# Two column groups in an output projection, staging rows on whole lines, and an expert stage's begin and end rearranged

## What is computed

```python
def _gated_head_norm(o, gate, w):
    of = o.astype(f32)
    y = of * lax.rsqrt(jnp.mean(of * of, axis=-1, keepdims=True) + EPS)
    return y * w.astype(f32) * jax.nn.silu(gate.astype(f32))
...
    o = _gated_head_norm(o, og.reshape(b_, L, H_A, DV_A), gnorm_w)
    return o.reshape(b_, L, DVT_A).astype(h.dtype) @ w_out, S_f, S_b
```

```python
        u = jnp.take(u_tab, idx, axis=0)
        act = jax.nn.gelu(jnp.einsum('td,ted->te', hc, u), approximate=False)
        coef = gates.astype(hc.dtype) * act
        vv = jnp.take(v_tab, idx, axis=0)
        return jnp.einsum('te,ted->td', coef, vv)
```

## Time and profile before

| | us |
|---|---|
| median of 3 runs (4644.31 to 4648.92) | 4647.11 |
| profiled execution | 4647.06 |
| its span | 4645.2 |
| span: mix_out layer 0, layer 1 | 730.6 to 855.3, 2914.3 to 3030.9 |
| span: experts layer 0, layer 1 | 1230.5 to 2452.7, 3406.6 to 4627.1 |
| PE busy | 4146.5 (89%) |
| DVE busy | 3803.5 (82%) |
| POOL, ACT busy | 1991.1 (43%), 1642.9 (35%) |

### The profile page before, as it was taken

The page is one execution under the profiler, slowest core; times in us unless marked ns, Lnnn a source line. Parts: engine busy times, 40 slices in busy tenths (PEclk is TensorE's granted clock), DMA queues, the critical chain, the costliest instruction groups (busy, mean ns, idle before and its releaser), DMA issues. The chain is left out here.

```text
span 4645.2 us, 72467 instructions
## 1 busy us (share of the span) xinstructions
PE 4146.5 (89%) x24511; PEld 3755.6 (81%) x24511; DVE 3803.5 (82%) x6733; ACT 1642.9 (35%) x2307; POOL 1991.1 (43%) x1435
## 2 busy tenths in 40 slices
PE   7799986877799999999996888786889999999997
PEld 3599986875699999999986778785779999999996
DVE  7688884599788888999996876378978888899997
ACT  7545442213233333333334432221323333333333
POOL 3234331215454545566544221220744545565663
PEclk9899998888899999999997988897999999999998
DMA  9411112214999999999972110220699999999995
GB/s 368 146 46 55 54 33 74 60 31 91 270 366 360 364 360 358 366 362 362 363 281 81 38 40 20 82 66 16 148 316 363 362 362 363 356 365 363 361 361 207
DMA packets 616027, 1049.49 MB, mean 226 GB/s; under 512 B 229699, under 2 KB 388870, under 8 KB 615430
## 3 DMA queue, kind: packets, MB, share of 16 engines
q1 hardware_dynamic: 467814, 508.86, 32.4%
q0 software_dynamic: 147456, 536.94, 31.1%
q10 hardware_dynamic: 672, 2.62, 0.2%
HBM read 982.75 MB, written 65.54 MB: 226 GB/s over the span
## 5 line engine op out<-in xcount | busy, mean ns | idle before, releaser
L1920 POOL DMA_INDIRECT rows_ex<-in_peer_v,ctx_index x512 | 707.6, 1382 | 475.5 <-DVE row_acc_ex L1999 359.9
L1920 POOL DMA_INDIRECT rows_ex<-in_peer_u,ctx_index x512 | 588.0, 1148 | 645.4 <-DVE dots_ex L2002 501.7
L2088 PE MATMUL pu_ex<-h_hi,uT_hi_ex 128*128 128x384 f32 x2048 | 715.6, 349 | 1.9 <-ACT coef_ex L1944 1.0
L1999 DVE SCALAR_TENSOR_TENSOR row_acc_ex<-rows_ex,factor_ex,row_acc_ex 128x1024 f32<-128x1024 f32 x512 | 657.6, 1284 | 52.8 <-issue 11.1
L2088 PE MATMUL pu_ex<-h_hi,uT_lo_ex 128*128 128x384 f32 x2048 | 692.6, 338 | 0.0
L2088 PE MATMUL pu_ex<-h_lo,uT_hi_ex 128*128 128x384 f32 x2048 | 692.5, 338 | 0.0
L2096 PE MATMUL py_ex<-v_hi_ex,c_hi_ex 128*128 128x512 f32 x1536 | 622.4, 405 | 0.0
L2002 DVE CUSTOM_DVE_ANT_0 rows_ex<-rows_ex,h_row_ex 128x1024 f32<-128x1024 f32 x512 | 604.3, 1217 | 0.0
L2096 PE MATMUL py_ex<-v_lo_ex,c_hi_ex 128*128 128x512 f32 x1536 | 601.0, 391 | 0.0
L2096 PE MATMUL py_ex<-v_hi_ex,c_lo_ex 128*128 128x512 f32 x1536 | 600.6, 391 | 0.0
L1933 ACT ACTIVATE uT_hi_ex<-pT_ex 128x512 fp32r<-128x512 f32 x512 | 304.1, 594 | 575.1 <-PE pT_ex L2081 473.0
(11 more groups left out here) (418 smaller groups left out, 8599.6 us busy)
## 6 DMA issues: line engine op xcount, KB each, us to landing
u_raw_ex<-in_peer_u SPq DMA_DIRECT2D x256, 512.0 KB
v_raw_ex<-in_peer_v SPq DMA_DIRECT2D x256, 512.0 KB
ada<-in_ada_w SPq DMA_DIRECT2D x24, 2048.0 KB, 10.0
gates<-stage_ro SPq DMA_DIRECT2D x12, 4096.0 KB, 23.3
g_raw_ex<-gates SPq DMA_DIRECT2D x256, 192.0 KB
w_raw_hgrn<-in_hgrn_w_in SPq DMA_DIRECT2D x40, 512.0 KB
w_raw_re<-in_peer_w_q SPq DMA_DIRECT2D x32, 512.0 KB, 3.7
w_raw_gla<-in_gla_w_in SPq DMA_DIRECT2D x25, 512.0 KB
```

What stands on the lines that cost most here:

```text
L1920: pool.indirect_dma_start(out=rows[m % RING][:, :], out_offset=None, in_=a["peer_u" if m < TG * NC else "peer_v"].rearrange("l n d -> (l n ...
L1999: nc.vector.scalar_tensor_tensor(row_acc[g][:, :], rows[j][:, :], factor[:, j:j + 1], row_acc[g][:, :], ALU.mult, ALU.add).then_inc(row_fr ...
L2088: last_ = nc.tensor.matmul(pu[:, 0:TD], w[:, k, :], x[:, k, 0:TD], start=(k == 0 and w is uT_hi[b] and x is h_hi), stop=(k == DC - 1 and w ...
```

## The change

`mix_out` takes two columns along in its loop over k instead of three. All squares and all sigmoids have buffers of their own, so the squares wait for nothing; the sums of squares, their inverses and roots are made in two groups of half the heads; there are two spread buffers, spread g + 2 standing behind head g's products. The gate's product with x and the norm weight (`gated`) is taken before the spread one, up to three chunks ahead. ACT issues all sigmoids ahead of the first root; SP loads gates 0 and 1 ahead of the weights. In `route` the `stage` buffers are allocated first. `experts` lets PE add the two parts of `h_row` by products with a rounded identity (`ident_r`, made in setup), ACT copies them, and PE's wait for that stands after the first turns. At its end the copies are shared 3 to 3 between ACT and DVE and PE starts after three of them, the turned rows have four buffers, and POOL's adds have no drain between them.

```diff
...
@@ -109,7 +109,7 @@
...
-            ("scale_w", [P, DC, 2], F32), ("lb", [P, 16], F32), ("oml", [P, 16], F32),
+            ("scale_w", [P, DC, 2], F32), ("ident_r", [P, P], F32R), ("lb", [P, 16], F32), ("oml", [P, 16], F32),
...
@@ -251,6 +251,8 @@
...
+            act.wait_ge(iot, 1)
+            act.activation(c["ident_r"][:, :], c["ident"][:, :], ACT.Copy)
...
@@ -1169,34 +1171,37 @@
...
-    AHEAD = 3
+    AHEAD = 2
+    GROUP = H // 2
...
-        sg = [sb(f"sg{i}", [P, T]) for i in range(2)]
-        sq = [sb(f"sq{i}", [P, T]) for i in range(2)]
+        sg = sb("sg", [P, DC, T])
+        sq = sb("sq", [P, DC, T])
...
-        spread_s = ps("spread_s", [P, 4, P])
-        spread_c = ps("spread_c", [P, P])
+        spread_s = [ps(f"spread_s{i}", [P, 4, P]) for i in range(2)]
+        spread_c = [ps(f"spread_c{i}", [P, P]) for i in range(2)]
...
-        rows = pp[0][0][:, 0:H * NT]
+
+        rows = [pp[j][0][:, 0:GROUP * NT] for j in range(2)]
+        inv = [c["inv"][:, j * GROUP * NT:(j + 1) * GROUP * NT] for j in range(2)]
 
         @block.sync
...
@@ -1208,10 +1213,9 @@
...
             gates(0)
+            gates(1)
             weights(0)
             weights(1)
-            gates(1)
-            weights(2)
             gates(2)
...
@@ -1228,14 +1232,11 @@
...
-            def gate(k):
+            for k in range(DC):
                 pool.wait_ge(sig_done, k + 1)
-                pool.tensor_tensor(og[:, k, :], og[:, k, :], sg[k % 2][:, :], ALU.mult).then_inc(gate_done, 1)
-
-            for k in range(DC):
-                gate(k)
-                if k < AHEAD:
-                    low(k)
+                pool.tensor_tensor(og[:, k, :], og[:, k, :], sg[:, k, :], ALU.mult).then_inc(gate_done, 1)
+                if k in (1, 2):
+                    low(k - 1)
...
@@ -1247,33 +1248,28 @@
...
-            def sigmoid(k):
+            for k in range(0, DC, 2):
+                act.activation(sq[:, k, :], oT[:, k, :], ACT.Square).then_inc(sq_act, 1)
+            for k in range(DC):
                 if k % 2 == 0:
                     act.wait_ge(og_in[k // 2], 16)
-                if k >= 2:
-                    act.wait_ge(gate_done, k - 1)
-                act.activation(sg[k % 2][:, :], og[:, k, :], ACT.Sigmoid).then_inc(sig_done, 1)
-
-            for k in range(0, DC, 2):
-                if k >= 2:
-                    act.wait_ge(summed, k - 1)
-                act.activation(sq[0][:, :], oT[:, k, :], ACT.Square).then_inc(sq_act, 1)
-            act.wait_ge(inverted, 1)
-            act.activation(inv, inv, ACT.Sqrt).then_inc(rooted, 1)
-            sigmoid(0)
-            high(0)
-            high(1)
-            sigmoid(1)
-            high(2)
-            for k in range(DC):
-                if k + 2 < DC:
-                    sigmoid(k + 2)
+                if k == 4:
+                    high(0)
+                    high(1)
+                act.activation(sg[:, k, :], og[:, k, :], ACT.Sigmoid).then_inc(sig_done, 1)
+            for j in range(2):
+                act.wait_ge(inverted, j + 1)
+                act.activation(inv[j], inv[j], ACT.Sqrt).then_inc(rooted, 1)
+                if j == 0:
+                    act.wait_ge(y_done, 1)
+                    act.activation(h_hi[:, 0, :], y[0][:, :], ACT.Copy).then_inc(hi_done, 1)
+            for k in range(1, DC):
...
@@ -1283,22 +1279,22 @@
...
         def _(pe):
-            for g in range(H):
+            def sums(g):
                 for k in range(g * NV, (g + 1) * NV):
                     pe.wait_ge((sq_act, sq_dve)[k % 2], k // 2 + 1)
                 for t in range(NT):
+                    col = g % GROUP * NT + t
                     for k in range(g * NV, (g + 1) * NV):
-                        last = nc.tensor.matmul(rows[:, g * NT + t:g * NT + t + 1], sq[k % 2][:, t * P:(t + 1) * P],
+                        last = nc.tensor.matmul(rows[g // GROUP][:, col:col + 1], sq[:, k, t * P:(t + 1) * P],
                                                 c["ones_d"][:, 0:1], start=(k % NV == 0), stop=(k % NV == NV - 1))
-                last.then_inc(summed, NV)
-            pe.wait_ge(rooted, 1)
+                last.then_inc(summed, 1)
...
             def spread(g):
-                if g:
-                    pe.wait_ge(spread_read, g)
+                pe.wait_ge(rooted, g // GROUP + 1)
                 for t in range(NT):
-                    dst = spread_s[:, t, :] if t < NT - 1 else spread_c[:, :]
-                    last = nc.tensor.matmul(dst, inv[:, g * NT + t:g * NT + t + 1].to_broadcast([P, P]),
+                    dst = spread_s[g % 2][:, t, :] if t < NT - 1 else spread_c[g % 2][:, :]
+                    col = g % GROUP * NT + t
+                    last = nc.tensor.matmul(dst, inv[g // GROUP][:, col:col + 1].to_broadcast([P, P]),
...
@@ -1310,18 +1306,24 @@
...
+            for g in range(GROUP):
+                sums(g)
             spread(0)
+            spread(1)
+            for g in range(GROUP, H):
+                sums(g)
             for k in range(DC):
-                if k % NV == NV - 1 and k // NV + 1 < H:
-                    spread(k // NV + 1)
-                if k == 0:
-                    pe.wait_ge(w_lo_done, AHEAD)
                 pe.wait_ge(lo_done, k + 1)
                 for j in range(AHEAD):
+                    if k == 0:
+                        pe.wait_ge(rooted, j + 1)
+                        pe.wait_ge(w_lo_done, j + 1)
                     for i, cols in halves():
                         last = terms(j, k, i, cols)
                         if k == DC - 1:
                             last.then_inc(proj, 1)
+                if k % NV == NV - 1 and k // NV + 2 < H:
+                    spread(k // NV + 2)
...
@@ -1332,45 +1334,55 @@
...
-            for k in range(1, DC, 2):
-                if k >= 2:
-                    dve.wait_ge(summed, k - 1)
-                nc.vector.tensor_mul(sq[1][:, :], oT[:, k, :], oT[:, k, :]).then_inc(sq_dve, 1)
-            dve.wait_ge(summed, DC)
-            nc.vector.tensor_scalar(inv, rows, float(D / mx.dv), EPS, ALU.mult, ALU.add)
-            dve.drain()
-            nc.vector.reciprocal(inv, inv)
-            dve.drain().then_inc(inverted, 1)
+            def gated(k):
+                dve.wait_ge(gate_done, k + 1)
+                nc.vector.scalar_tensor_tensor(oT[:, k, :], oT[:, k, :], c["vec"][:, gw + k % NV:gw + k % NV + 1],
+                                               og[:, k, :], ALU.mult, ALU.mult)
+
+            def inverse(j):
+                dve.wait_ge(summed, (j + 1) * GROUP)
+                nc.vector.tensor_scalar(inv[j], rows[j], float(D / mx.dv), EPS, ALU.mult, ALU.add)
+                dve.drain()
+                nc.vector.reciprocal(inv[j], inv[j])
+                dve.drain().then_inc(inverted, 1)
 
             def normal(k):
                 g = k // NV
                 dve.wait_ge(spread_done, g + 1)
-                by = (spread_s[:, :, :].rearrange("p t n -> p (t n)"), spread_c[:, :])
+                by = (spread_s[g % 2][:, :, :].rearrange("p t n -> p (t n)"), spread_c[g % 2][:, :])
                 for v, cols in parts():
-                    last = nc.vector.scalar_tensor_tensor(y[k % 3][:, cols], oT[:, k, cols],
-                                                          c["vec"][:, gw + k % NV:gw + k % NV + 1], by[v],
-                                                          ALU.mult, ALU.mult)
-                if k % NV == NV - 1:
-                    last.then_inc(spread_read, 1)
+                    last = nc.vector.tensor_tensor(y[k % 3][:, cols], oT[:, k, cols], by[v], ALU.mult)
+                last.then_inc(y_done, 1)
...
+            for k in range(1, DC, 2):
+                nc.vector.tensor_mul(sq[:, k, :], oT[:, k, :], oT[:, k, :]).then_inc(sq_dve, 1)
+            dve.wait_ge(sq_act, DC // 2)
+            dve.wait_ge(sq_dve, DC // 2)
+            gated(0)
+            gated(1)
+            inverse(0)
+            gated(2)
+            dve.drain()
             for k in range(DC):
                 normal(k)
-                dve.wait_ge(gate_done, k + 1)
-                dve.drain()
-                nc.vector.tensor_mul(y[k % 3][:, :], y[k % 3][:, :], og[:, k, :]).then_inc(y_done, 1)
+                if k == 0:
+                    inverse(1)
+                if k + 3 < DC:
+                    gated(k + 3)
                 if k >= 1:
                     low(k - 1)
+                dve.drain()
             low(DC - 1)
             dve.wait_ge(x_in, 16)
...
@@ -1577,6 +1589,7 @@
...
+        stage = [sb(f"stage{i}", [P, KEYS, STORE]) for i in range(2)]
...
@@ -1596,7 +1609,6 @@
...
-        stage = [sb(f"stage{i}", [P, KEYS, STORE]) for i in range(2)]
...
@@ -1875,14 +1887,19 @@
...
+        def turned_rows(k):
+
+
+            return (pu, pT[:, 0, :]) if k % 4 == 0 else (py[2 * (k % 4) - 2], py[2 * (k % 4) - 1])
...
@@ -1923,8 +1940,9 @@
...
                 pool.wait_ge(squared, k + 1)
```

(50 more changed lines are left out.)

19 lines of the change are left out of this document (9 added, 10 removed).

## The result

| | before | changed |
|---|---|---|
| median, us | 4647.7 | 4603.8 |
| lowest to highest | 4644.3 to 4648.9 | 4598.9 to 4607.1 |
| span of the profiled execution | 4645.2 | 4596.8 |

What follows compares the result with a forecast made beforehand. The experts' loop keeps the tensor engine busy 200 of 200 us beside a DMA share of 0.97 and stays; only stage ends move. 22 + 0.5 + 11.3 + 2.8 + 3.5 = 40.1 off 4647.11 gives 4607, own range 4601 to 4614.

Steps and rivals of the forecast that it cites:

- Route: Route's stores: aligned 256 B rows land sooner, ACT stops waiting; 11.1 and 10.6 us, sum 22, between 0 and 23.
- what ends last: Route's end, layer 0: last store lands at 1217.8, DVE's second look-up ends at 1218.2, then 1.2 for the barrier.
- The lower bound: Route's packet price: 13.6 ns for an aligned 256 B, from the projection's 512 B weight rows at 27.1 ns.
- Projection, layer 0: Output projection, layer 0: later first product, shorter turns, six columns instead of five; gain 0.5 us, between -2 and 2.5.
- Projection, layer 1: Output projection, layer 1: gates near 2926, root 2929, turns at DVE's 2.7; gain 11.3 us, between 8 and 12.
- same chain of DVE: Projection, layer 1: DVE's work between the forty sums (to 2943) and the first product, put at 2948.9.
- Rival D: Projection's loop over k: clock does not rise, turns 7.8 and 3.2, total 4635; chance 0.06.
- Experts' begin: Experts' start: 32 accumulating products at 0.217 replace DVE's adds; 1.4 us a layer, sum 2.8, between 0 and 8.
- Experts' end: Experts' end: two ACT copies instead of four, POOL's adds without drains; sum 3.5 us, up to 18.
- the drain that moves: Experts' end: the 7.3 us is paid by POOL's first drain behind the gathers, now the block's own; 1.8 gained; forecast's chance 0.46.
- the one that vanishes: Experts' end, rival A: the first drain's 7.3 us belongs to its place and goes; 14.5 more, 4592; chance 0.26.
- Rival C: Experts' loop becomes bound by DMA at a lower rate, slower than before; 4703 at 7% lower; chance 0.03.

Runs made afterwards that it cites:

- 19.2 alone: Kernel before with one edit, route's stage buffers allocated first: 4629.4 us, ratio 0.9953.
- its second: The changed kernel itself, unaltered, timed and traced once more: 4598.4 us, ratio 0.9896.
- the edit alone: Kernel before with only the output projection's (`mix_out`) edits: 4632.9 us, ratio 0.9964; looked at again, 4631.4, ratio 0.9957.
- the two kernels with `low` first: Changed kernel with DVE's low(k - 1) ahead of gated(k + 3): 4596.4 us; the same plus early drain on POOL and early first root: 4570.7.
- the experiment: Changed kernel with one more POOL drain right behind its last gather: 4590.3 us, ratio 0.9874.
- the three offset kernels: Kernel before with route's stage first but its rows 64, 128 or 224 B past a multiple of 256: 4649.1, 4648.1 and 4648.6 us.

## Why the prediction was right, point by point

The forecast 4607 stood 3 us above 4603.8, and the mechanisms of route and of the drain held. That it came so close is in part luck. Between the traces the projection gained 22.4 against 11.8 forecast, the experts 2.6 against 6.3, route 21.3 against 22, all else 2.1 against nothing: 48.4 against 40.1, of which the medians keep 43.9.

- **Route**, forecast 22, measured 21.3 in the traces, 19.2 alone. Price of a packet 13.6 forecast, 14.1 measured; store 15.4 to its landing forecast, 15.9 measured; what ends last was the pair forecast. The lower bound was taken from 512 B rows, which turned out the right neighbour.
- **Projection, layer 0**, forecast 0.5 (-2 to 2.5). Against the one trace before it gained 5.5 in the changed kernel's first trace, 2.2 in its second, -1.8 with the edit alone; against traces that entered the stage alike 5.5, 0.8 and -0.3. Two of these three lie within the bounds, and the first trace, by which the kernel's result was read, does not. The term that was mis-sized is the price of the second group of sums: 0.217 each, the price at the low clock, 8.7 in all. It was right for the edit alone (8.5); in the changed kernel the clock was up for 3.3 us as they began, and they took 5.5. Root: 17.2 us into its stage forecast, 16.2 measured. (The terms given for it, 743, two sigmoids and 1.28, reach only 745.7 and not 747.8. In the trace the third pair of gates is in at 739.98, and two splits of weights, 2.0, and four sigmoids, 2.6, follow before the table load.) First product 34.6 forecast, 30.5 measured. From there to the first of the six columns 43.0 forecast, 42.6 measured.
- **Projection, layer 1**, forecast 11.3 (8 to 12), measured 16.9 and, with the edit alone, 16.3, outside its bounds. First product 34.6 forecast, 31.3 measured: the same sums (5.6 instead of 8.7, in all five traces of this code), 0.7 less on the spreads and 1.9 less on DVE, against a root that came 2.5 later than I had it. Behind the 1.9 is a slip: the "same chain of DVE" is 3.7 us in layer 0 (761.5 to 765.2) and 5.9 in layer 1 (2943 to 2948.9), and it measures 4.1 in both. The turns take 2.5 and not 2.7 (DVE rows 0.69 and 0.28 for `normal`, where I had taken 0.75 and 0.34 of the three-operand form); with the gap ahead of the columns 24.6 forecast, 22.3 measured.
- **Rival D** (the clock stays low in the emptier loop), given 0.06, did happen in part: three turns at 7.0 to 7.4 us in layer 0, where I had two, and four in the second trace. The clock of us 30 to 60 is lower than with the old code in two of the three rows of the table above (0.75 for 0.86, 0.68 for 0.79), and the two kernels with `low` first, whose turns are shorter, have 0.92 and 0.96.
- **Experts' begin**, forecast 1.4 a layer, measured 1.3 and 0.6. The price 0.217 was right: 32 products in 6.9 us (1214.37 to 1221.23), at a granted clock of 0.50.
- **Experts' end**, forecast 1.8 a layer, measured 1.2. PE's turns start 0.9 sooner (1.0 forecast) and the gap behind the adds is 8.6 (8.9 forecast); but the adds stand 1.68 apart and not 1.55, 0.8 in all: each waits for the one before (the 0.15 in the brackets of its row). The choice between the drain that moves and the one that vanishes (0.46 against 0.26) was right, by the reason given, and the experiment made it a gain of its own.
- **Rival C** did not occur: DMA share 0.98 at 362 GB/s in the loop, PE 170 of 170 us busy.

## What to carry to other kernels

A store of short rows is worth a look at where the rows begin: list the sizes of the tiles in front of it, and put the one that transfers small rows first. When a wait is fixed to "the first of its kind" (here POOL's first drain behind its gathers), removing the instruction that shows it only moves it; put one where the engine is idle anyhow. When PE's clock changes inside a stage, one price per instruction is not enough: cost PE's pieces at both levels, take more than one trace of both kernels, and set a trace against one that entered the stage at the same clock.

## What the runs showed of the hardware

- A transfer of 256 B rows from SBUF costs 14.1 ns a packet (290 GB/s) where each row is one line of 256 B, and 18.8 (217 GB/s) where it crosses into the next, the same at 64, 128, 160 and 224 B into the line.
- With the crossing rows SP's instruction that issues a store is longer itself: 2.1 us in the median and up to 3.4 in the three offset kernels, 2.2 and up to 4.0 in the kernel before, against 0.37 aligned. Nothing stood behind it on SP here.
- POOL's first drain behind its gathers takes 8.7 us from the last gather's end when it stands right there, and 7.3 when 24 or 33 us have passed; later ones in the stage cost at most 0.1 beyond the add before them (1.61 for 1.54).
- PE's granted clock at the start of layer 0's projection, and with it 3 to 7 us, differs between traces whose instructions there are the same (119.4 twice, 122.7, and 126.7 and 126.8 in the kernel with that part alone; with the old code 123.5 to 126.5). They go with the clock of the stage's first 10 us; why that differs stays open.
